# Two chained blocks on one core: GLA's output among RWKV's projections, and a new order of VectorE's work in the RWKV scan

## The chip, the cores and the metric

One core of a Trainium2 chip (trn2) runs the whole program in one launch. The metric is the device time of that launch in microseconds (us), the median of several runs. Times inside the program come from one profiled execution of the kernel before.

## What is computed

Two blocks run one after the other on 1024 tokens of 1024 channels in float32. Only the mixer of the first block matters here. It projects the normed tokens and gives half of the channels to a bidirectional gated linear attention (GLA, 4 heads) and half to a bidirectional RWKV-7 scan (8 heads), and concatenates the two:

```python
z = xn @ w_in[i]
z_rwkv, z_gla = z[..., :RWKV_IN_WIDTH], z[..., RWKV_IN_WIDTH:]
z_rwkv = z_rwkv + rwkv_mu[i] * (centred_shift(z_rwkv) - z_rwkv)
y_rwkv = rwkv7_mixer(z_rwkv, ...)      # two scans over time, S = S*w + (S@-kk) b^T + v k^T
y_gla = gla_mixer(z_gla, ...)          # ends with: o = rms_norm(o_f + o_b, norm_w) * silu(g)
y = jnp.concatenate([y_rwkv, y_gla], axis=-1) @ w_out[i]
```

The second block takes shifts and gains from a vector c through a 1024x6144 matrix ("ada" below); that product depends on nothing of the first block.

## The kernel before, in words

Each engine (PE = TensorE, DVE = VectorE, ACT = ScalarE, POOL = GpSimd, SP, which issues most transfers) runs its own instruction stream, written out by hand stage by stage. Every instruction counts up a semaphore of its engine, and `wait_ge` in front of an instruction holds the engine, with all that stands behind it, until named instructions or transfers are done. `meet` makes all engines wait for the ends of a stage. The stages around the change are `gla_scan`, `gla_out`, `rwkv_in` and `rwkv_scan`.

**GLA's output** (`gla_out_*`). The four heads' sums o lie in `g_o` (channels on partitions, 1024 tokens in the free dimension). ACT squares a head into one of two buffers `g_tmp`; PE sums it over the channels with two-column matmuls, 16 trace rows a head (`token_sums_pe`, L697). DVE and ACT form the inverse roots (`rsqrt_dve`, `rsqrt_act`). Then per head: DVE spreads the roots (`over_dve`, L685), PE turns them with eight 128x128 transposes into PSUM banks 6 and 7 (`over_pe`, L691), DVE multiplies o by norm and gate (L1159, L1161). All this is ahead of the stage's `meet`, and SP then stores `g_o` to DRAM as one transfer, `y_gla`.

**RWKV's projections** (`rwkv_in_*`). Fifteen blocks of the weight matrix, block j in two halves of 512 tokens, are multiplied on PE with operands split in a high and a low part: 24 matmuls for (j, 0) and 24 for (j, 1) (`split_pe`, L642 to L644). The weights come through a ring of three (SP, L594); ACT makes the high part of block j+2 behind PE's block j (`third_high_act`), DVE the low part (`third_low_dve`, L607), then reads block j out of PSUM, and shifts and mixes it with three more passes over 1024 tokens. Blocks 0 to 2 give `r_wlo`, `r_alo` and `r_sglo`. Between the halves PE does the jobs of the table `RJOBS`: ("sg", n) from (2, 1) on are decay products into banks 6 and 7, which DVE reads and ACT puts through a sigmoid; ("kk_sums", 0) at (7, 1) are 64 trace rows of two-column matmuls on the squared keys, the last square being made by ACT behind block 7.

ACT and POOL also work at ada in this stage, units q = 32 to 95: ACT scales a 128x512 piece of the matrix (L2532), POOL adds it to the sum (L2543), and ACT's next unit waits for that addition. ACT does the units of block j at the end of its work for j: `32 + 64*j//14` to `32 + 64*(j+1)//14`, so 4 or 5 a block from j = 0 on. Their buffers `aw` overlap `g_o`, so ACT first waits for the transfer `y_gla`. Behind (3, 1) PE sums the first finished group of eight, units 32 to 39 (`ada_sum_pe`, L2554, from the table `groups`), behind (5, 1) units 40 to 47, behind (6, 1) units 48 to 55.

**The RWKV scan** (`rwkv_scan_*`). 16 chunks of 64 tokens, 4 heads and both directions d at once. A turn u of the loop overlaps three chunks: the recurrence for u, the level products for m = u + 1, the Gram matrices for n = u + 2, and DVE's scaled operands for u + 3. The 64x64 triangular inverse of a chunk is made in steps. DVE masks the Gram matrices (`nm`, `mm`, L1717). The 16x16 diagonal blocks go by DRAM into `N16` on 32 partitions, and DVE inverts them in 15 levels of two short instructions (`substitute_dve`, L1673 and L1674), ahead of which it copies the identity (L1659). The result goes by DRAM into `ZZ` one turn later. Two more levels join 16 to 32 and 32 to 64: PE `p4`, DVE mask `t4` (L1737), PE `l4`, DVE `zz` (L1743), PE `p5`, DVE mask `t5` (L1750), PE `l5`, DVE `xt` (L1756). Transfers, in SP's order in a turn: `nm` out, then `ZZ` of the chunk before in (POOL issues half), `N16` in (POOL issues some), and later the inverted blocks out. DVE's order in a turn is: state update `S` (waits for PE's `ss`), masks, decay of S, y in the second half, products of u + 3 for d = 0, `t4`, products for d = 1, `zz`, identity and levels 0 and 1, `t5`, levels 2 to 4, `xt`, levels 5 to 14.

Of the kernel before, what the change touches and what calls it, by code (L numbers as in the profile page):

```python
# [211 lines left out]
class Kernel:  # L212
# [116 lines left out]
    def plan_block1(self):  # L329
# [225 lines left out]
    def pool_program(self):  # L555
# [583 lines left out]
    def gla_out_act(self):
        act = self.act  # L1140
        for h in range(4):
            if h >= 2:
# [2 lines left out]
        self.rsqrt_act("go", 64)
        for j in range(2):
            self.third_high_act("r", self.rw, self.rwkv_blocks(), j)
        self.meet(act, "gla_out")

    def gla_out_dve(self):  # L1150
        dve = self.dve
        self.rsqrt_dve("go", 64, [self.pe["go_sums", 3]], ALU.mult, 1.0 / PART, ALU.add, 1e-6)
        for h in range(4):
            y = self.g_o[:, h, :]
            if h >= 2:
                dve.wait_ge(self.pe["go%d" % (h - 2), "over"])
            self.over_dve("go%d" % h, self.st[:, 1, 16 * h:16 * h + 16].rearrange("p (b two) -> p b two", two=2)[:, :, 0:1], self.g_tmp[:, h % 2, :])
            dve.wait_ge(self.pe["go%d" % h, "over"])
            dve.c.scalar_tensor_tensor(out=two(y), in0=two(y), scalar=self.col("gla_norm"), in1=self.ps[:, 6:8, :], op0=ALU.mult, op1=ALU.mult) \  # L1159
                .then_inc(*dve.one("go", h))  # L1160
            dve.c.tensor_tensor(y, y, self.g_gate[:, h, :], ALU.mult).then_inc(*dve.one())  # L1161
# [144 lines left out]
    def rwkv_in_act(self):  # L1306
# [3 lines left out]
        act.wait_ge(self.t_keep["y_gla"])  # L1310
        for q in range(32, 36):
            self.ada_load_act(q)
        for j in range(15):
# [57 lines left out]
    def rwkv_in_dve(self):  # L1371
# [1882 lines left out]
```

## Time and profile before

| what | us |
|---|---|
| median of 3 runs | 3611.45 (3607.79 to 3614.22) |
| profiled execution, its own time | 3603.32 |
| its span, first to last instruction | 3602.0 |
| GLA's output, first sum to first projection | 419.29 to 458.71 |
| projections, up to the scan's first product | 458.71 to about 706 |
| RWKV scan | about 706 to 1106 |

The profile's times are microseconds from the first instruction. In a timeline row the first number is the start and the second the busy time of the row's instructions together ("x8" are eight); in brackets stands how long the engine stood idle before it and for whom. Matmul rows overlap, since they are pipelined. A float32 matmul shows as more than one row of the trace.

### The profile page before, as it was taken

Reading aid. Unit: us, or ns where it says so; the run is one execution under the profiler, and the core shown is the slowest. Engines: PE = TensorE matmul, PEld = TensorE weight load, DVE = VectorE, ACT = ScalarE, POOL = GpSimd, SP = SyncE. Lnnn points to the kernel's source line nnn. Section 1 sums busy time; section 2 is a strip of 40 time slices with the busy share of each in tenths; the row PEclk is TensorE's granted clock in tenths of the full one; section 3 lists DMA queues with packets and bytes.
Section 4 is the critical chain, followed back from the end, with each engine's and each line's share of the span. In section 5 each row is a group of like instructions: output and inputs, shape, how many; then the busy total and the mean of one; then the engine's idle time right before and its main releaser. Section 6 shows DMA issues by size and latency. Waiting matters only on the chain.

```text
span 3602.0 us, 56544 instructions
## 1 busy us (share of the span) xinstructions
PE 3262.9 (91%) x24603; PEld 2709.9 (75%) x24603; DVE 2270.9 (63%) x3114; ACT 1003.5 (28%) x1482; POOL 466.9 (13%) x362
## 2 busy tenths in 40 slices
PE   7988789888886999999999888998888899999996
PEld 5777767778885778888888667876676678888885
DVE  5758555678786444444444667996556566666666
ACT  4544233312113221111111452124454211211112
POOL 2520023322224000000000310000001001111110
PEclk9988698999998999999999999999999999999999
DMA  4410054322213111111110212122001111111111
GB/s 135 124 50 14 16 168 132 90 41 39 38 30 131 58 42 53 53 36 53 53 53 24 95 52 65 36 58 68 1 1 59 35 41 48 57 49 47 47 47 65
DMA packets 242719, 207.27 MB, mean 58 GB/s; under 512 B 66744, under 2 KB 205127, under 8 KB 241959
## 3 DMA queue, kind: packets, MB, share of 16 engines
q1 hardware_dynamic: 223527, 176.96, 16.4%
q10 hardware_dynamic: 13824, 25.17, 2.2%
q0 software_dynamic: 5120, 1.53, 0.4%
q8 instruction: 193, 3.16, 0.4%
q14 instruction: 55, 0.45, 0.0%
HBM read 172.06 MB, written 29.64 MB: 56 GB/s over the span
## 4 chain that ended last, share of the span: by engine, by line
PE 55%; DVE 8%; ACT 4%; issue 1%; POOL 0%; DMA 0%; DVEq 0%; SPq 0%; ACTq 0%; POOLq 0%
PE ps L2168 23%; PE ps L2183 16%; PE ps L2031 5%; PE ps L2916 2%; DVE Yc L2793 2%; PE ps L2892 2%; PE ps L642 1%; PE ps L643 1%; PE ps L644 1%; PE ps L2902 1%; PE ps L2893 1%; DVE e L2004 1%; ACT e L1986 0%; DVE small L1997 0%; POOL o_l L1780 0%
## 5 line engine op out<-in xcount | busy, mean ns | idle before, releaser
L3210 DVE TENSOR_TENSOR H<-H,ps 128x1024 f32<-128x1024 f32 x256 | 312.7, 1221 | 181.0 <-PE ps L2183 174.1
L2333 DVE TENSOR_TENSOR fsum<-fsum,ps 128x1024 f32<-128x1024 f32 x168 | 205.2, 1221 | 312.4 <-PE ps L2183 310.3
L2183 PE MATMUL ps<-dh,hh 128*128 128x512 f32 x864 | 339.9, 393 | 20.2 <-DVE hl L2148 14.2
L2183 PE MATMUL ps<-dl,hh 128*128 128x512 f32 x864 | 338.3, 392 | 0.0
L2183 PE MATMUL ps<-dh,hl 128*128 128x512 f32 x864 | 338.1, 391 | 0.0
L2168 PE MATMUL ps<-hn_h,uh 128*128 128x512 f32 x704 | 275.8, 392 | 7.2 <-DVE ul L1780 4.8
L2168 PE MATMUL ps<-hn_l,uh 128*128 128x512 f32 x704 | 275.3, 391 | 0.0
L2168 PE MATMUL ps<-hn_h,ul 128*128 128x512 f32 x704 | 275.3, 391 | 0.0
L2168 PE MATMUL ps<-hx_h,uh 128*128 128x512 f32 x512 | 200.5, 392 | 8.5 <-DVE hx_l L2148 5.3
L2183 PEld LDWEIGHTS ps<-dh,hh 128*128 128x128 f32 x864 | 163.7, 189 | 58.6 <-DVE hl L2148 15.9
L2168 PE MATMUL ps<-hx_l,uh 128*128 128x512 f32 x512 | 199.9, 390 | 0.0
L2168 PE MATMUL ps<-hx_h,ul 128*128 128x512 f32 x512 | 199.9, 390 | 0.0
L2183 PEld LDWEIGHTS ps<-dh,hl 128*128 128x128 f32 x864 | 163.5, 189 | 34.3
L2183 PEld LDWEIGHTS ps<-dl,hh 128*128 128x128 f32 x864 | 163.6, 189 | 33.6
L2543 POOL TENSOR_TENSOR a_x<-a_x,a_t 128x512 f32<-128x512 f32 x84 | 129.0, 1536 | 337.8 <-ACT a_t L2532 234.2
L3180 POOL TENSOR_TENSOR dw<-dw,g_row 128x1024 f32<-128x1024 f32 x32 | 78.7, 2461 | 707.4 <-DMA dw<-in_w_mlp_dram 707.4
L2168 PEld LDWEIGHTS ps<-hn_h,uh 128*128 128x128 f32 x704 | 133.1, 189 | 35.6 <-DVE ul L1780 5.2
L2793 DVE SCALAR_TENSOR_TENSOR Yc<-cp,cols,Yc 128x1024 f32<-128x1024 f32 x120 | 154.2, 1285 | 4.3
L2168 PEld LDWEIGHTS ps<-hn_l,uh 128*128 128x128 f32 x704 | 133.1, 189 | 27.7
L2168 PEld LDWEIGHTS ps<-hn_h,ul 128*128 128x128 f32 x704 | 133.0, 189 | 27.9
L642 PE MATMUL ps<-hx_h,cw 128*128 128x512 f32 x320 | 130.8, 409 | 17.2 <-DVE cw L622 7.5
L3189 ACT ACTIVATE relu<-ps 128x1024 f32<-128x1024 f32 x32 | 32.9, 1029 | 406.2 <-PE ps L2168 406.2
(474 smaller groups left out, 7626.8 us busy)
## 6 DMA issues: line engine op xcount, KB each, us to landing
aw<-in_w_ada_dram ACTq DMA_DIRECT2D x96, 256.0 KB, 3.0
uw<-in_w_mlp_dram SPq DMA_DIRECT2D x32, 512.0 KB, 4.2
dw<-in_w_mlp_dram SPq DMA_DIRECT2D x32, 512.0 KB, 5.1
uw<-in_ffn_gate_dram SPq DMA_DIRECT2D x22, 512.0 KB, 4.0
uw<-in_ffn_up_dram SPq DMA_DIRECT2D x22, 512.0 KB, 5.3
dw<-in_ffn_down_dram SPq DMA_DIRECT2D x22, 512.0 KB, 5.9
cw<-in_w_in_dram SPq DMA_DIRECT2D x20, 512.0 KB, 3.9
o_w<-in_w_out_dram SPq DMA_DIRECT2D x16, 512.0 KB, 9.9
```

The lines of the kernel that those rows point to most:

```text
L642: pe.e.matmul(ps[0:m, 2 * (j % 2) + h, :], wh[:, k, :], xh, start=(k == 0), stop=False)
L643: pe.e.matmul(ps[0:m, 2 * (j % 2) + h, :], wh[:, k, :], xl, start=False, stop=False)
L2031: mm = pe.e.matmul(self.ps[:, 2 * (t % 2) + hf, :], x[a](k), w[b](k)[:, half(hf)], start=(n == 0 and m == 0), stop=(n == len(order) - 1 an ...
L2168: mm = pe.e.matmul(ps[:, 2 * pair + h, :], w[:, col], x[h][v][:, k, :], start=(k == 0 and m == 0), stop=(k == DC - 1 and m == 2))
L2183: mm = pe.e.matmul(ps[:, 2 * pair + hf, :], v[s][:, blk(t)], w[:, half(hf)], start=(m == 0), stop=(m == 2))
L2333: return dve.c.tensor_tensor(f, f, new, ALU.add) if g else dve.c.tensor_copy(f, new)
L2543: pool.c.tensor_tensor(acc[:], acc[:], self.a_t[who][:], ALU.add).then_inc(*pool.one("ada", q, who))
L2793: dve.c.scalar_tensor_tensor(out=o, in0=x[:, w:w + TOK], scalar=self.col("dw", n + 4 * w), in1=o, op0=ALU.mult, op1=ALU.add) \
L2892: pe.e.matmul(ps[:, b, :], self.Qb[:, u, :], self.kr[:, u % 4, key:key + self.K8], start=True, stop=True)
L2916: mm = pe.e.matmul(ps[:, 6, blk(pr)], self.PT[u % 2][:, blk(j)], v, start=(j == 0), stop=(j == 5))
L3180: pool.e.tensor_tensor(w, w, self.g2_row[:], ALU.mult).then_inc(*pool.one("m", "dw", g))
L3210: return dve.c.tensor_tensor(h, h, self.ps[:, 4 + 2 * (t % 2):6 + 2 * (t % 2), :], ALU.add)
```

## The change

**GLA's output.** The stage's `meet` goes. Ahead of the projections PE keeps only the sums of heads 0 and 1. The sums of heads 2 and 3 stand behind (0, 0), and the four transposes of the inverse roots behind (0, 1), (1, 0), (1, 1) and (2, 0), in the order of heads 3, 0, 1, 2. DVE's products follow in `rwkv_in_dve`: one head ahead of block 0, two behind its mixing, the last behind the reading of block 1. ACT makes the high parts of blocks 0 and 1 between the squares. SP loads `r_wup` and `r_w0` behind the second head, and stores `y_gla` in its turn j = 1, behind the fourth. ACT waits for `y_gla` at the end of its work for j = 2, and then does units 32 to 40, nine of them, and five for each block after; `groups` stays. The first sg job waits for the fourth head. A third shift buffer `r_sh1` serves block 1.

**Scan.** On DVE both directions' products stand ahead of `t4`, and the identity copy too (`identity_dve`). The substitution starts behind `t5`: levels 0 to 3, then `xt`, then 4 to 14.

```diff
     def gla_out_pe(self):
-        for h in range(4):
-            pe.wait_ge(self.act["go_sq", h])
-            self.token_sums_pe(...)
-        for h in range(4):
-            if h:
-                pe.wait_ge(self.dve["go", h - 1])
-            self.over_pe("go%d" % h, NBLK, self.g_tmp[:, h % 2, :])
-        self.meet(pe, "gla_out")
+        for h in range(2):
+            self.gla_sums(h)
...
+    def gla_gated_dve(self, p):
+        dve, h = self.dve, self.GOUT[p]
+        y = self.g_o[:, h, :]
+        dve.wait_ge(self.pe["go%d" % p, "over"])
+        dve.c.scalar_tensor_tensor(... in1=self.ps[:, 6:8, :] ...).then_inc(*dve.one("go", p))
+        dve.c.tensor_tensor(y, y, self.g_gate[:, h, :], ALU.mult).then_inc(*dve.one("gated", p))
+        if p < 2:
+            self.gla_wide_dve(p + 2)
...  rwkv_in_sp
-        self.meet(sp, "gla_out")
-        sp.e.dma_start(self.dram["y_gla"], self.g_o[:]).then_inc(*self.t_keep.one("y_gla"))
+        sp.wait_ge(self.dve["gated", 1])
...
+            if j == 1:
+                sp.wait_ge(self.dve["gated", 3])
+                sp.e.dma_start(self.dram["y_gla"], self.g_o[:]).then_inc(*self.t_keep.one("y_gla"))
...  rwkv_in_pe
-            if (j, h) == (0, 1):
+            if (j, h) == (0, 0):
                 self.over_pe("xr", NBLK, self.r_sh[0][:])
+                for k in (2, 3):
+                    self.gla_sums(k)
+            elif j < 2 or (j, h) == (2, 0):
+                self.gla_over_pe(2 * j + h - 1)
...  rwkv_in_act
-        act.wait_ge(self.t_keep["y_gla"])
-        for q in range(32, 36):
-            self.ada_load_act(q)
+        self.rsqrt_act("go", 64)
...
-            for q in range(32 + 64 * j // 14, 32 + 64 * (j + 1) // 14 if j < 14 else 0):
+            if j == 2:
+                act.wait_ge(self.t_keep["y_gla"])
+                for q in range(32, 36):
+                    self.ada_load_act(q)
+            for q in range(32 + 64 * (j - 1) // 13 if j > 2 else 32, 32 + 64 * j // 13 if 2 <= j < 14 else 0):
                 self.ada_act(q)
...  rwkv_scan_dve
-            if u + 3 < NSUB:
-                products(u + 3, 0)
+            for d in range(2):
+                if u + 3 < NSUB:
+                    products(u + 3, d)
+            if n < NSUB:
+                self.identity_dve(n)
...
-            if n < NSUB:
-                self.substitute_dve(n, 0, 2)
...
-                self.substitute_dve(n, 2, 5)
+                self.substitute_dve(n, 0, 4)
...
-                self.substitute_dve(n, 5, 15)
+                self.substitute_dve(n, 4, 15)
```

Two places of the order of instructions. ACT from the end of GLA's output, before (`r_inv` is the copy behind the first transposes, `rwh` a block's high part, `aw` a load of an ada piece, `a_x` and `a_t` ada units):

```order
L1309 ACTIVATE r_inv_146<-ps 128x1024
L2520 DMA aw_59<-in_w_ada_dram 128x512
L2520 DMA aw_60<-in_w_ada_dram 128x512
L2520 DMA aw_61<-in_w_ada_dram 128x512
L2520 DMA aw_62<-in_w_ada_dram 128x512
L2145 ACTIVATE rwh_128<-rwr_127 128x1024
L2532 ACTIVATE a_x_63<-aw_59,cc_55 128x512
L2520 DMA aw_59<-in_w_ada_dram 128x512
```

And now, from the high part of block 2 on:

```order
L2172 ACTIVATE rwh_128<-rwr_127 128x1024
L2172 ACTIVATE rwh_129<-rwr_125 128x1024
L1333 ACT_TABLE_LOAD
L1333 ACTIVATE r_wlo_145<-r_wlo_145 128x1024
L2172 ACTIVATE rwh_128<-rwr_126 128x1024
L1301 ACT_TABLE_LOAD
L1301 ACTIVATE r_sg_149<-r_sg_149 128x1024
L2547 DMA aw_59<-in_w_ada_dram 128x512
L2547 DMA aw_60<-in_w_ada_dram 128x512
L2547 DMA aw_61<-in_w_ada_dram 128x512
L2547 DMA aw_62<-in_w_ada_dram 128x512
L2559 ACTIVATE a_x_63<-aw_59,cc_55 128x512
```

The loads of ada pieces, which stood ahead of everything for the blocks, now stand behind three high parts, the tanh of `r_wlo` and the first sigmoid of `r_sg`.

DVE in a turn of the scan, before, from `t4` on (`s_T` is `t4` or `t5`; `s_AR`, `s_BK`, `s_F`, `s_last` the products; `s_tmp` and `s_Z` the substitution):

```order
L1737 TENSOR_TENSOR s_T_172<-ps,lev_mask_161 128x256 [waits pe] x2
L1697 TENSOR_TENSOR s_F_178<-s_last_179,s_Ei_163 128x4 [waits dve]
L1698 TENSOR_TENSOR s_AR_182<-r_kk_143,s_Ex_165 128x4x64
L1699 TENSOR_TENSOR s_BK_196<-r_bb_142,s_En_164 128x4x64
L1700 TENSOR_TENSOR s_AR_182<-r_rkv_124,s_Ei_163 128x4x64
L1701 TENSOR_TENSOR s_BK_196<-r_rkv_124,s_En_164 128x4x64
L1702 COPY s_last_179<-s_Ei_163 128x4 [waits dve]
L1743 TENSOR_TENSOR s_ZZ_143_191<-s_ZZ_187,ps 128x512 [waits pe] x2
L1659 COPY s_Z_144_192<-eye_118_166 32x2x256 [waits dve,t_z]
L1673 TENSOR_TENSOR s_tmp_127_175<-s_N_119_167,s_Z_144_192 32x30 [waits dve,t_nb,t_n]
L1674 TENSOR_TENSOR s_Z_144_192<-s_Z_144_192,s_tmp_127_175 32x2x15 [waits dve]
L1673 TENSOR_TENSOR s_tmp_127_175<-s_N_119_167,s_Z_144_192 32x56 [waits dve]
```

And now, from the products of d = 1 on:

```order
L1726 TENSOR_TENSOR s_F_179<-s_last_180,s_Ei_164 128x4 [waits dve,pe]
L1727 TENSOR_TENSOR s_AR_183<-r_kk_144,s_Ex_166 128x4x64
L1728 TENSOR_TENSOR s_BK_197<-r_bb_143,s_En_165 128x4x64
L1729 TENSOR_TENSOR s_AR_183<-r_rkv_124,s_Ei_164 128x4x64
L1730 TENSOR_TENSOR s_BK_197<-r_rkv_124,s_En_165 128x4x64
L1731 COPY s_last_180<-s_Ei_164 128x4 [waits dve]
L1681 COPY s_Z_145_193<-eye_119_167 32x2x256 [waits dve,t_z]
L1769 TENSOR_TENSOR s_T_173<-ps,lev_mask_162 128x256 [waits pe] x2
L1773 TENSOR_TENSOR s_ZZ_144_192<-s_ZZ_188,ps 128x512 [waits pe] x2
L1777 TENSOR_TENSOR s_T_173<-ps,lev_mask_162 128x256 [waits pe] x2
L1702 TENSOR_TENSOR s_tmp_128_176<-s_N_120_168,s_Z_145_193 32x30 [waits t_nb,dve,t_n]
L1703 TENSOR_TENSOR s_Z_145_193<-s_Z_145_193,s_tmp_128_176 32x2x15 [waits dve]
```

The six products and the identity copy have moved from behind the first `s_T` to ahead of it, and the second `s_T` from behind two levels to ahead of all.

## Rows read from the trace of the kernel before

**Rows 1.** The page's first part: busy time, share of the span, instructions.
```profile
PE 3262.9 (91%) x24603; PEld 2709.9 (75%) x24603; DVE 2270.9 (63%) x3114; ACT 1003.5 (28%) x1482; POOL 466.9 (13%) x362
```

**Rows 2.** Windows: stretch, its us; PE, PEld, DVE, ACT, POOL busy; granted clock; DMA.
```profile
418.00:433.00 15.00, 13.71 (x64) 13.72 (x64) 0.00 (x0) 5.40 (x5) 0.00 (x0) 0.50 0.38 87
...
708.00:1075.00 367.00, 319.49 (x8176) 303.38 (x8175) 288.30 (x917) 69.61 (x148) 93.00 (x156) 0.96 0.21 38
```

**Rows 3.** Timeline of PE, GLA's output and the first projections.
```profile
419.29 13.78 PE L697 MATMUL ps<-ones,g_tmp 128*128 128x2 f32 x64 [2.16 <-ACT g_tmp L1144]
436.10 1.97 PE L691 MATMUL ps<-ident,g_tmp 128*128 128x128 f32 x8 [3.03 <-DVE g_tmp L685]
...
458.71 0.77 PE L642 MATMUL ps<-xs_h,rwh 128*128 128x512 f32 x1 [4.46 <-DVE rwl L607]
...
471.93 1.03 PE L691 MATMUL ps<-ident,r_sh 128*128 128x128 f32 x8
```

**Rows 4.** Timeline of DVE, the first head of GLA's output.
```profile
438.11 1.28 DVE L1159 SCALAR_TENSOR_TENSOR g_o<-g_o,cols,ps 128x1024 f32<-128x1024 f32 x1 [2.06 <-PE ps L691]
439.42 1.22 DVE L1161 TENSOR_TENSOR g_o<-g_o,g_gate 128x1024 f32<-128x1024 f32 x1
```

**Rows 5.** Timeline of ACT: loads, first ada unit, a table load, eighth unit.
```profile
473.11 1.79 ACTq L2520 DMA_DIRECT2D aw<-in_w_ada_dram  x4
...
476.75 0.73 ACT L2532 ACTIVATE a_x<-aw,cc 128x512 f32<-128x512 f32 x1 [0.74 <-DMA aw<-in_w_ada_dram]
...
485.65 1.28 ACT L1321 ACT_TABLE_LOAD   x1
...
495.24 0.72 ACT L2532 ACTIVATE a_t<-aw,cc 128x512 f32<-128x512 f32 x1 [1.50 <-POOL a_x L2543]
```

**Rows 6.** Timeline of PE in the projections: first ada sum, kk_sums.
```profile
509.02 0.95 PE L2554 MATMUL ps<-ones,a_x 128*128 128x2 f32 x8
...
577.57 7.63 PE L1245 MATMUL ps<-r_hsel,r_kk 128*128 128x2 f32 x35 [7.14 <-ACT r_kk L1328]
```

**Rows 7.** Timeline of DVE, one turn of the scan.
```profile
849.51 1.27 DVE L1717 TENSOR_TENSOR s_NM<-ps,gram_mask 128x512 f32<-128x512 f32 x2
...
857.02 0.89 DVE L1737 TENSOR_TENSOR s_T<-ps,lev_mask 128x256 f32<-128x256 f32 x2 [2.53 <-PE ps L1486]
...
859.56 1.28 DVE L1743 TENSOR_TENSOR s_ZZ<-s_ZZ,ps 128x512 f32<-128x512 f32 x2
...
862.32 0.74 DVE L1750 TENSOR_TENSOR s_T<-ps,lev_mask 128x256 f32<-128x256 f32 x2
...
864.66 0.73 DVE L1756 TENSOR_TENSOR s_XT<-s_ZZ,ps 128x256 f32<-128x256 f32 x2
...
873.05 0.42 DVE L1712 TENSOR_TENSOR s_S<-s_S,ps 128x256 f32<-128x256 f32 x1 [1.32 <-PE ps L1486]
```

**Rows 8.** DVE's `nm` masks over the scan: ns min/median/max, first and last start.
```profile
L1717 DVE TENSOR_TENSOR s_NM<-ps,gram_mask x32: 661/676/692, 709.8 to 1063.5; 128x512 f32<-128x512 f32 x32
```

**Rows 9.** Waits, 730 to 1060: who for whom, us in total, times, longest.
```profile
DVE s_T L1737 <- PE ps L1486: 34.9, 14, 3.8
...
DVE s_S L1712 <- PE ps L1486: 6.7, 9, 1.4
```

**Rows 10.** Transfers: destination, issuing queue, count, KB each, median us to landing.
```profile
rwr<-in_w_in_dram SPq DMA_DIRECT2D x14, 512.0 KB, 4.4
...
y_gla_dram<-g_o SPq DMA_DIRECT2D x1, 2048.0 KB, 8.1
```

**Rows 11.** Timeline of PE, start of `p4` in the next turn.
```profile
880.91 1.15 PE L1486 MATMUL ps<-s_ZZ,s_NM 64*64 64x64 f32 x32 [0.31 <-DMA s_ZZ<-zd_dram]
```

**Rows 12.** Timeline of DVE, the turn that has no products left.
```profile
1070.28 0.89 DVE L1737 TENSOR_TENSOR s_T<-ps,lev_mask 128x256 f32<-128x256 f32 x2 [3.63 <-PE ps L1486]
...
1072.93 0.69 DVE L1743 TENSOR_TENSOR s_ZZ<-s_ZZ,ps 128x512 f32<-128x512 f32 x1 [0.25 <-PE ps L1589]
...
1074.52 0.19 DVE L1673 TENSOR_TENSOR s_tmp<-s_N,s_Z 32x30 f32<-32x30 f32 x1 [0.38 <-DMA s_N<-nd_dram]
```

More of the change, by code:

```diff
@@ L1144, in gla_out_act, with gla_wide_dve @@
             act.e.activation(self.g_tmp[:, h % 2, :], self.g_o[:, h, :], ACTF.Square).then_inc(*act.one("go_sq", h))
[L1145 to L1148, printed above, removed]
-    def gla_out_dve(self):
[L1151 to L1161, printed above, removed]
+            if h % 2:
+                self.third_high_act("r", self.rw, self.rwkv_blocks(), h // 2)
+    def gla_wide_dve(self, p):
+        h = self.GOUT[p]
+        self.over_dve("go%d" % p, self.st[:, 1, 16 * h:16 * h + 16].rearrange("p (b two) -> p b two", two=2)[:, :, 0:1], self.g_tmp[:, p % 2, :])
+    def gla_gated_dve(self, p):
+        dve, h = self.dve, self.GOUT[p]
+        y = self.g_o[:, h, :]
+        dve.wait_ge(self.pe["go%d" % p, "over"])
+        dve.c.scalar_tensor_tensor(out=two(y), in0=two(y), scalar=self.col("gla_norm"), in1=self.ps[:, 6:8, :], op0=ALU.mult, op1=ALU.mult) \
+            .then_inc(*dve.one("go", p))
+        dve.c.tensor_tensor(y, y, self.g_gate[:, h, :], ALU.mult).then_inc(*dve.one("gated", p))
+        if p < 2:
+            self.gla_wide_dve(p + 2)
+    def gla_out_dve(self):
         for j in range(2):
             self.third_low_dve("r", self.rw, self.rwkv_blocks(), j)
-        self.meet(dve, "gla_out")
     RJOBS = {(2, 1): ("sg", 0), (3, 0): ("sg", 1), (3, 1): ("sg", 2), (4, 0): ("sg", 3), (4, 1): ("sg", 4), (5, 0): ("sg", 5), (5, 1): ("sg", 6), (6, 0): ("sg", 7),
@@ L1378, in rwkv_in_dve @@
         dve.e.tensor_scalar(self.r_omka[:], self.cols[:, ka:ka + 4], -1.0, 1.0, ALU.mult, ALU.add).then_inc(*dve.one())
-        dve.wait_ge(self.act["xr_inv"])
+        self.rsqrt_dve("go", 64, [self.pe["go_sums", 3]], ALU.mult, 1.0 / PART, ALU.add, 1e-6)
+        for p in range(2):
+            self.gla_wide_dve(p)
+        self.gla_gated_dve(0)
         for j in range(15):
             dst, mu, rows = self.rwkv_dst(j)
-            z, s = self.r_zp[j % 2], self.r_sh[j % 2]
+            z, s = self.r_zp[j % 2], self.r_sh[j % 2] if j != 1 else self.r_sh1
             dve.wait_ge(self.pe["r", j])
@@ L1397, in rwkv_in_dve @@
                 .then_inc(*dve.one("r_sh", j))
+            if j == 0:
+                self.gla_gated_dve(1)
+                self.gla_gated_dve(2)
             if j in (4, 6, 7, 9, 11, 12, 14):
@@ L1650, in rwkv_scan_pool, with identity_dve @@
         self.meet(self.pool, "rwkv_scan")
+    def identity_dve(self, n):
+        dve = self.dve
+        if n:
+            dve.wait_ge(self.t_z["out", n - 1])
+        dve.c.tensor_copy(self.Z16[:, :, 1], self.eye16[:]).then_inc(*dve.one("one", n))
     def substitute_dve(self, n, first, end):
@@ L1656, in substitute_dve @@
         if first == 0:
-            if n:
-                dve.wait_ge(self.t_z["out", n - 1])
-            dve.c.tensor_copy(self.Z16[:, :, 1], self.eye16[:]).then_inc(*dve.one())
+            dve.wait_ge(dve["one", n])
             dve.wait_ge(self.t_n["in", n], self.t_nb["in", n])
@@ L1737, in rwkv_scan_dve @@
                     dve.e.tensor_tensor(self.T[:, L[d]], self.hb(d, 0), rep(self.lev_mask[:, 0, d], 4), ALU.mult).then_inc(*dve.one("t4", m, d))
-            if u + 3 < NSUB:
-                products(u + 3, 1)
             if 0 <= m < NSUB:
```

19 lines of the change are left out of this document (14 added, 5 removed).

## The prediction

> **What bounds the kernel now.** I read the page's busy shares first: PE has work in 91% of the span [rows 1], so a change pays where PE idles or runs slowly. The windows show such stretches [rows 2]: during GLA's sums the granted clock is 0.50 (1.2 GHz); in the scan it is 0.96, and PE is busy 319 of 367 us. The timelines then say what the waits are for.
>
> *GLA's output.* PE starts the sums at 419.29 and the first projection at 458.71 [rows 3]. The 64 two-column rows take 13.8 us, 3.44 a head, and then the heads' transposes start 5.4 us apart: transposes 1.97, two products on DVE of 1.28 and 1.22, the rest spreading and hand-overs [rows 3, 4]. All of it lies on the path to the end.
>
> *Projections.* PE is dense, but ACT and POOL are nearly as full with ada. The first unit starts at 476.75, 3.6 us after the first load was issued, the eighth at 495.24 [rows 5]. PE's sum of these eight stands at 509.02 and waits for nothing; only ahead of kk_sums (577.57) does PE wait, 7.1 us for ACT, and the rows that follow have a pitch of 0.22 us, where the ada sum's have 0.11 [rows 6]: the half clock and the full one.
>
> *Scan.* A turn is a ring: `nm` is masked, SP fetches `ZZ`, PE makes `p4`, DVE masks `t4` and goes through ladder and substitution to S and the next `nm`. In the turn shown `nm` ends at 850.8, `t4` starts at 857.0 after 2.53 of idle time, and S could start at 871.7 but waits for PE to 873.05 [rows 7]. The masks go from 709.8 to 1063.5 over 15 turns, 23.6 us each [rows 8]. In 14 turns DVE waits 34.9 us ahead of `t4` and 6.7 ahead of S [rows 9].
>
> **GLA's output, step by step.** PE now does two heads ahead of the first projection: 2 x 3.44 from 419.3, so it starts at 426.2, if the weights are there. Their load is issued at 418.1 and lands in some 4.4 us [rows 10], high and low part take another 2.3: 424.8, in time. **Gain 32.5 us.** Then PE takes part of it back. Eight transposes at full clock show 1.03 us, 0.8 in pitch [rows 3]; four sets come into the projections, 3.2. The 32 sum rows cost 3.5 at the full clock's pitch [rows 6]. For a clock that falls there I add 2; the bounds are 0 and 5.8 (3.4 for the sums at the half clock, 2.4 for the start of a half block), and that GLA's 64 sums stay at 0.50 although they stand back to back [rows 2] says that such rows don't raise it.
>
> The Trainium skill (TensorE: Matmul & The Clock Gate, Part 4: PE-mode transpose) says that a transpose doesn't count as a busy PE. The eight at 471.93 run at full clock between dense matmuls, those at 436.10 take 1.97, which fits the rule without proving it. By the rule this term would be its upper bound, 5.8.
>
> **Who waits in between.** (0, 0) starts slowly as before and ends near 434, the sums near 440, (0, 1) near 446; a half block takes 5.5 (458.71 to 471.93 for block 0 [rows 3], less 2.4 for its slow start, halved). DVE's first head ends at 449.4, block 0 takes it 7.0 (low part, reading and three passes), the second head 2.5 [rows 4]: 458.9. Only then does SP issue the last small loads (3 us) and the fourth weight load. That lands at 466.4; high part, low part and reading of block 1 take 3.6, the fourth head 2.5: 472.6. PE loses 0.2 us at the first sg job and 2.2 at the second, and without ada would be behind (3, 1) at 486.8, where it was at 509.0: 22 us ahead.
>
> **There the lead is lost.** `y_gla` is issued at 472.7 and lands 8.1 us later [rows 10], at 480.8. ACT gets there at 481.2 and starts the first unit 3.6 us behind: 484.8. From the first to the eighth it was 18.5 us; I take off 2.3 for a table load (1.28) and a tanh that no longer stand between [rows 5]: 501.0, and POOL adds till 502.5. `groups` still asks for these eight behind (3, 1). So PE idles from 486.8 to 502.5 and keeps **6.5 us**. The nearest row for this is the old ada sum at 509.02; the units behind are chained one by one as before. Units 48 to 55 end with j = 5, and PE waits some 6 us more behind (6, 1), but that costs nothing: ACT's chain decides when kk_sums starts, 571 against 577.57. There the wait of 7.1 us goes, since PE has only just come through its block, and the 64 rows begin at the full clock. Half of them at 0.11 and not 0.22 is 3.5 us; the bounds are 0 and 7. Behind kk_sums nothing changes.
>
> **Output and projections together: 6.5 + 3.5 = 10 us less.** The low bound is 0, if `y_gla` or ACT is later by 7 to 10 us; the high one 23, if PE waited nowhere for ada (32.5 - 3.2 - 3.5 - 2, and 1 for the rest).
>
> **Scan, step by step.** No work is added. Ahead of `t4` go the products of d = 1 (1.6 us) and the identity copy (0.5), into an idle time of 2.5 on average [rows 9]: they are hidden by it, and would delay `t4` one for one if it were gone; I count 0.1. `t4` doesn't come earlier, as `p4` waits for `ZZ` [rows 11]. The turn without products shows the bare ladder: `zz` ends 3.34 behind the start of `t4` [rows 12], against 3.8 [rows 7]. `p5` of the second direction takes 0.6 and 0.15 of hand-over, `t5` 0.4: it ends at 4.5, before at 6.04. Then come four levels (2.0), `xt` (0.75), the fifth level (0.6) and what stood behind `xt` (865.4 to 871.7, 6.3): S can start 14.2 behind `t4`, before 14.7. PE starts `l5` 1.9 us earlier and is in time with `ss`, so that the 6.7 us ahead of S go. 14 x 0.5 + 6.7 = 13.7; the other way, a turn becomes 6.2 (to `t4`) + 14.2 + 1.95 (S and `nm`) = 22.35, 17.5 less over 14 turns. I take **14 us**. Bounds: 3, if the new waits for `l4` and `p5` are as long as the old one (2.5; of the ladder's 4.5 us DVE is busy 3.0), and 18. More is not to be had: the substitution needs `N16`, which came 10.4 us behind `nm` [rows 12], and now starts at 10.7.
>
> **The sum.** 10 + 14 = 24 us. From the profiled execution's 3603.3 that gives 3579.3. That execution is 8.1 us below the median of the runs; set against the median the forecast is 3611.4 - 24 = **3587 us**.
>
> **Rivals.**
>
> *A. The scan's new waits eat its gain.* For it: DVE now has nothing between `t4` and `zz`, and PE's slower moments all show. Against it: rows 12 have 0.25 of waiting for the second `zz`. 3611.4 - 10 - 3 = 3598.
>
> *B. The projections give nothing.* For it: ACT's ada chain starts 8 us later than before (484.8 for 476.75) and has to make it up; blocks with five units take 2.2 more than those with four. Against it: nine units now run in one piece. 3611.4 - 14 = 3597; with A as well 3608, no change.
>
> *C. The change doesn't meet a wait at (3, 1)*, because POOL adds faster than I read. All 23 us stay: 3611.4 - 37 = 3574. That the units wait for each other speaks against it.
>
> *D. Slower: PE's clock in the scan.* PE is busy 20.5 us a turn (319 of 367) at 0.96. At a granted clock g it takes 19.7/g, and some 3 of gaps come with the ladder. For it: the idle time gathers in fewer, longer pieces, and after one the clock has fallen before [rows 6]. It decides from the g at which the turn grows by the projections' 10 us over 14, to 24.3: 19.7/21.3 = 0.92. At 0.85 the turn is 26.2, 2.6 over today's, 36 us in all: 3611.4 - 10 + 36 = 3638. Against it: PE's idle time a turn shrinks by what the turn does.
>
> **How the numbers follow.** Forecast 0.48, A 0.15, B 0.14, A and B together 0.08, C 0.08, D 0.07. The predicted time is the forecast's. The range goes from 3570 (the high bounds of both parts, 41 us) to 3606 (2 or 3 us left of each), and leaves out D and half of A with B. Less than about 0.2%, 7.2 us, a measurement of this kernel can't tell from no change. Forecast, A, B and C lie beyond it, 0.85, of which 0.04 for their near ends falls within: faster 0.81, within 0.2% 0.12, slower 0.07.
>
> **What would show it.** Right: first projection near 426; the ada sum behind (3, 1) released by POOL near 502 after some 15 us; `y_gla` issued near 473; kk_sums near 571 without its wait, first rows at 0.11; in the scan `t5` ending 4.5 behind `t4`, no wait ahead of S, masks 22.4 to 22.6 apart. Wrong: no wait at (3, 1) (C), kk_sums still near 577 (B), 2.5 us a turn of waits for `zz` and `t5` (A), a clock in the scan below 0.92 (D).

## The result and the profile after

| | before | changed |
|---|---|---|
| median of the runs, us | 3607.79 (3605.29 to 3614.22, 5 runs) | 3590.73 (3584.53 to 3596.08, 5 runs) |
| ratio, 95% interval | | 0.9950, 0.9933 to 0.9967 |
| span of the profiled execution, us | 3602.0 | 3583.2 |
| mean granted clock | 0.948 | 0.949 |

The change saves 17 us, about 0.5%. (The median of before now includes two runs taken beside the changed kernel.) The forecast was 24 less, 3587 against the earlier median of 3611.45; the time measured lies in its range. Why 17 and not 24 is what follows.

The busy shares say little [rows 1]: the work is the same, and so are the shares.

```profile
PE 3261.7 (91%) x24603; PEld 2701.1 (75%) x24603; DVE 2268.1 (63%) x3114; ACT 1003.2 (28%) x1482; POOL 464.1 (13%) x362
```

TensorE's timeline of the changed kernel answers to rows 3 and 6. Line 697 are two-column sums, 642 the first matmul of a projection, 691 transposes, 1244 the sg jobs, 2581 the sums of ada's units, 1255 kk_sums (its row holds only the matmuls up to 580, the end of the window asked for).

```profile
415.58 6.96 PE L697 MATMUL ps<-ones,g_tmp 128*128 128x2 f32 x32 [2.16 <-ACT g_tmp L1152]
422.40 0.77 PE L642 MATMUL ps<-xs_h,rwh 128*128 128x512 f32 x1
...
429.52 1.03 PE L691 MATMUL ps<-ident,r_sh 128*128 128x128 f32 x8
430.39 3.63 PE L697 MATMUL ps<-ones,g_tmp 128*128 128x2 f32 x32
433.88 0.48 PE L642 MATMUL ps<-xs_h,rwh 128*128 128x512 f32 x1
...
474.84 1.13 PE L1244 MATMUL ps<-r_wup,r_wlo 64*128 64x512 f32 x4 [1.71 <-DVE r_sg L1358]
...
494.66 1.87 PE L2581 MATMUL ps<-ones,a_x 128*128 128x2 f32 x8 [13.03 <-POOL a_x L2570]
496.46 2.08 PE L1244 MATMUL ps<-r_wup,r_wlo 64*128 64x512 f32 x4
...
545.41 1.87 PE L2581 MATMUL ps<-ones,a_x 128*128 128x2 f32 x8 [5.56 <-POOL a_x L2570]
...
568.50 11.81 PE L1255 MATMUL ps<-r_hsel,r_kk 128*128 128x2 f32 x57 [2.19 <-ACT r_kk L1340]
```

The first sum stands 3.7 us earlier than before (415.58 for 419.29) although nothing ahead of it was changed, so I count from it. The first projection comes 6.8 behind it, before 39.4. The sum of ada's first eight units, now ahead of its data, waits 13 us for GpSimd, and the matmuls behind it (1.87 for 0.95, 2.08 for 1.13) run at the half clock. kk_sums starts 152.9 us behind the first sum, before 158.3: 5.4 of the 32.5 us are left. TensorE itself is ready for it 150.7 us behind the first sum, before 151.1; what has shrunk is its wait for ScalarE, from 7.1 us [rows 6] to 2.2. The rows of kk_sums still have a pitch of 0.21.

The windows of TensorE: stretch, its us, PE busy, granted clock, DMA share and GB/s.

```profile
427.00:434.00 7.00, 7.00 (x53) 1.00 0.01 2
...
560.00:590.00 30.00, 27.81 (x121) 0.72 0.22 63
701.00:1043.00 342.00, 305.54 (x7908) 0.98 0.22 38
```

Through the transposes and sums between the half blocks the clock stayed whole in this execution; around kk_sums it is 0.72, in the scan 0.98 for 0.96 [rows 2].

In the scan, the row of VectorE's `nm` masks answers to rows 8. They span 341.7 us against 353.7, 22.8 a turn for 23.6.

```profile
L1746 DVE TENSOR_TENSOR s_NM<-ps,gram_mask x32: 661/669/692, 701.3 to 1043.0; 128x512 f32<-128x512 f32 x32
```

VectorE's waits from 700 to 1045, for rows 9. Line 1769 is level four's mask `t4`, 1773 `zz`, 1777 level five's mask `t5`:

```profile
DVE s_ZZ L1773 <- PE ps L1613: 16.6, 28, 1.4
DVE s_T L1777 <- PE ps L1510: 6.2, 14, 0.5
DVE s_T L1769 <- PE ps L1510: 5.2, 9, 1.3
```

The 34.9 us ahead of `t4` have shrunk to 5.2 and the 6.7 ahead of S are gone, while 22.8 have appeared in the ladder. In all, 13.6 us of waiting less. One turn on VectorE's timeline, for rows 7:

```profile
842.71 0.89 DVE L1769 TENSOR_TENSOR s_T<-ps,lev_mask 128x256 f32<-128x256 f32 x2 [0.28 <-PE ps L1510]
844.43 0.69 DVE L1773 TENSOR_TENSOR s_ZZ<-s_ZZ,ps 128x512 f32<-128x512 f32 x1 [0.82 <-PE ps L1613]
845.36 0.69 DVE L1773 TENSOR_TENSOR s_ZZ<-s_ZZ,ps 128x512 f32<-128x512 f32 x1 [0.24 <-PE ps L1613]
...
846.83 0.42 DVE L1777 TENSOR_TENSOR s_T<-ps,lev_mask 128x256 f32<-128x256 f32 x1 [0.45 <-PE ps L1510]
847.39 0.19 DVE L1702 TENSOR_TENSOR s_tmp<-s_N,s_Z 32x30 f32<-32x30 f32 x1
...
856.89 0.73 DVE L1741 TENSOR_TENSOR s_S<-s_S,ps 128x256 f32<-128x256 f32 x2
857.56 1.26 DVE L1746 TENSOR_TENSOR s_NM<-ps,gram_mask 128x512 f32<-128x512 f32 x2
```

`t5` ends 4.5 us behind the start of `t4`, and S starts 14.2 behind it. Read so in all turns, S starts 14.14 to 14.19 us behind `t4` in 14 of 15 (15.5 in one), where before it was 14.4 to 16.0, 15.04 on average.

So the stretches give 3.7 us that are not the change's, 4.8 in the projections (285.7 us from the first sum to the first mask, before 290.5) and 12.0 in the scan, and 1.7 are lost behind it (2540.2 us for 2538.5, where the executions below scatter from 2537.1 to 2541.5 with the same code); 18.8 in all, the difference of the spans. The change's own part is some 17.

### The profile page after: what moved, and what is told of

Its sections match the earlier page's. It is cut to its first block, busy times and chain, and to the rows that moved or that the text cites. A ratio compares the mean times of both kernels' runs of the same rounds, so it can differ in the third digit from the quotient of the medians.

```text
span 3583.2 us, 56554 instructions
## 1 busy us (share of the span) xinstructions
PE 3261.7 (91%) x24603; PEld 2701.1 (75%) x24603; DVE 2268.1 (63%) x3114; ACT 1003.2 (28%) x1482; POOL 464.1 (13%) x362
## 4 chain that ended last, share of the span: by engine, by line
PE 56%; DVE 8%; ACT 4%; issue 1%; POOL 0%; DMA 0%; DVEq 0%; SPq 0%; ACTq 0%; POOLq 0%
PE ps L2195 23%; PE ps L2210 16%; PE ps L2058 5%; PE ps L2943 2%; DVE Yc L2820 2%; PE ps L2919 2%; PE ps L642 1%; PE ps L643 1%; PE ps L644 1%; PE ps L2929 1%; PE ps L2920 1%; DVE e L2031 1%; ACT e L2013 0%; DVE small L2024 0%; POOL o_l L1807 0%
## 5 line engine op out<-in xcount | busy, mean ns | idle before, releaser
L2210 PE MATMUL ps<-dh,hh 128*128 128x512 f32 x864 | 340.8, 394 | 17.9 <-DVE hl L2175 14.2
L2195 PE MATMUL ps<-hn_h,ul 128*128 128x512 f32 x704 | 275.3, 391 | 0.0
```

The source lines that it names most:

```text
L2195: mm = pe.e.matmul(ps[:, 2 * pair + h, :], w[:, col], x[h][v][:, k, :], start=(k == 0 and m == 0), stop=(k == DC - 1 and m == 2))
L2210: mm = pe.e.matmul(ps[:, 2 * pair + hf, :], v[s][:, blk(t)], w[:, half(hf)], start=(m == 0), stop=(m == 2))
```

## The experiments

Each experiment's profile is read by the same four stretches. Times in us; the ratio is to the kernel before, run beside it on the same chip.

| kernel | median | ratio (95%) | first sum at | from it to first mask | first to last mask | behind |
|---|---|---|---|---|---|---|
| before | 3607.8 | | 419.3 | 290.5 | 353.7 | 2538.5 |
| changed | 3590.7 | 0.9950 (0.9933 to 0.9967) | 415.6 | 285.7 | 341.7 | 2540.2 |
| e1 scan only | 3590.3 | 0.9958 (0.9941 to 0.9976) | 411.7 | 291.4 | 341.3 | 2541.5 |
| e2 output only | 3602.0 | 0.9995 (0.9980 to 1.0009) | 424.7 | 285.7 | 350.8 | 2538.8 |
| e3 sums later | 3586.5 | 0.9942 (0.9921 to 0.9963) | 421.2 | 285.0 | 347.7 | 2538.5 |
| e4 units spread | 3579.6 | 0.9930 (0.9909 to 0.9952) | 418.3 | 275.3 | 341.8 | 2540.5 |
| e5 load 3 first | 3578.9 | 0.9929 (0.9908 to 0.9949) | 418.5 | 280.4 | 341.5 | 2537.1 |
| e6 load 3, spread | 3572.6 | 0.9908 (0.9890 to 0.9927) | 424.1 | 268.8 | 341.2 | 2541.3 |
| e7 products only | 3589.0 | 0.9954 (0.9937 to 0.9972) | 419.7 | 285.7 | 340.0 | 2539.5 |
| e8 substitution only | 3604.3 | 0.9995 (0.9984 to 1.0006) | 425.0 | 285.7 | 355.8 | 2537.7 |
| e9 all three | 3569.8 | 0.9904 (0.9888 to 0.9920) | 420.7 | 266.7 | 339.9 | 2541.2 |
| e10 changed again | 3591.5 | 0.9958 (0.9941 to 0.9974) | 420.8 | 288.1 | 345.0 | 2540.2 |

The first column of stretches is noise: up to there all these kernels do the same, and it goes from 411.7 to 425.0.

**The two parts, each alone.** e1 is the kernel before with the scan's new order of VectorE, e2 the changed kernel with the old one.

> The kernel before, with only the scan's new order on VectorE. Theory (the two parts of the change are independent, and the scan gives most of it): the trace of the changed kernel shows 341.7 us from the first to the last mask of N where the kernel before has 353.7, so this kernel is 12 us faster than before (ratio 0.9967), masks 22.8 us apart, the first mask still near 709.8. Rival (the scan profits from what the projections leave behind, its clock or its transfers): masks stay over 23.2 us apart here and the gain is under 6 us.

> The changed kernel with the scan's old order, so only GLA's output is moved. Theory: 4.8 to 5.4 us less than before (ratio 0.9986), counted from GLA's first sum to the first mask of N; masks stay 23.6 us apart. In the changed kernel's trace the first sum itself stood 3.7 us earlier than before; if that belongs to one execution, it is somewhere between 415 and 419 here and the time tells nothing of it; if it belongs to the change, the sum is at 415.6 again and the gain is 8 to 9 us (0.9977). Rival: the projections give nothing, within 2 us of before.

e1 has the changed kernel's scan to half a microsecond (341.3) and, within the intervals, its whole gain. e2 has the changed kernel's first stretch exactly (285.7, 4.8 under before), but its time can't be told from before: the interval runs from 7 us less to 3 us more. So the scan gives most, the two are independent, and what the first part gives is seen in the trace alone. The 12 us of the scan are good to some 3: its old order spans 353.7 us in one execution and 350.8 in the other (e2, which I had expected at 23.6 a turn and which has 23.4), its new order 341.2 to 347.7 in the seven that have it unchanged. e2's first sum at 424.7 also settles that the earlier sum of the changed kernel belonged to one execution.

**What TensorE waits for at (3, 1).** First the sums alone are put later:

```
-        groups = dict(zip((3, 5, 6, 8, 10, 11, 13), range(4, 11)))
+        groups = dict(zip((4, 6, 7, 9, 10, 12, 13), range(4, 11)))
...
-            if j in (4, 6, 7, 9, 11, 12, 14):
+            if j in (5, 7, 8, 10, 11, 13, 14):
```

> The changed kernel with TensorE's sums of ada's units put one half block or more later: groups behind blocks 4, 6, 7, 9, 10, 12, 13 in place of 3, 5, 6, 8, 10, 11, 13. Theory 1 (the sum at (3, 1) is what TensorE waits for, nothing else is late there): the waits of 13.0 and 5.6 us for GpSimd are gone, and kk_sums starts 8 us earlier or more: 8 us less than the changed kernel, near 3583. Theory 2 (ScalarE's chain is the limit: the nine units of block 2 stand ahead of the high part of block 5, and VectorE's sg work comes behind): the wait of 13 us turns into waits at the next sg jobs and for the weights of block 5, and kk_sums moves by less than 4 us: 0 to 4 us less than the changed kernel.

The wait of 13 us went and came back 12.2 us long at the sg job right behind, now for VectorE. e3's TensorE, at the old place and at kk_sums (cut off at 580 again):

```profile
509.16 2.08 PE L1244 MATMUL ps<-r_wup,r_wlo 64*128 64x512 f32 x4 [12.23 <-DVE r_sg L1358]
...
572.62 7.63 PE L1255 MATMUL ps<-r_hsel,r_kk 128*128 128x2 f32 x35 [5.86 <-ACT r_kk L1340]
```

kk_sums moved from 152.9 to 151.4 us behind the first sum. That is the second theory: the data of that sum is only the first of several things that hang on ScalarE. ScalarE's timeline in the changed kernel shows the order: the high part of block 3, the loads of ada, nine units from 478 to 494, and only then the sigmoid of sg1 and the high part of block 5.

```profile
461.23 1.06 ACT L2172 ACTIVATE rwh<-rwr 128x1024 fp32r<-128x1024 f32 x1 [20.52 <-DMA rwr<-in_w_in_dram]
...
474.82 1.78 ACTq L2547 DMA_DIRECT2D aw<-in_w_ada_dram  x4
478.09 0.72 ACT L2559 ACTIVATE a_x<-aw,cc 128x512 f32<-128x512 f32 x1 [2.22 <-DMA aw<-in_w_ada_dram]
...
492.55 0.72 ACT L2559 ACTIVATE a_t<-aw,cc 128x512 f32<-128x512 f32 x1 [1.43 <-POOL a_x L2570]
...
494.81 1.06 ACT L1301 ACTIVATE r_sg<-r_sg 128x1024 f32<-128x1024 f32 x1 [0.41 <-ACT a_x L2559]
495.77 1.04 ACT L2172 ACTIVATE rwh<-rwr 128x1024 fp32r<-128x1024 f32 x1
```

e4 therefore deals the units out as well:

```
+    UNITS = (32, 32, 36, 41, 46, 52, 57, 62, 68, 73, 78, 84, 90, 96)
...
-            for q in range(32 + 64 * (j - 1) // 13 if j > 2 else 32, 32 + 64 * j // 13 if 2 <= j < 14 else 0):
+            for q in range(self.UNITS[j - 1], self.UNITS[j]) if 2 <= j < 14 else ():
```

> As the run before, with ScalarE's units of ada dealt out differently: 4 behind block 2 in place of 9, then 5 or 6 a block. Theory 2 (ScalarE's order is the limit at (3, 1)): the high part of block 5 comes 10 us earlier, the waits at (3, 1) and at the sg jobs behind it fall under 4 us together, and kk_sums starts 4 to 10 us earlier than in the changed kernel, as far as the six units a block further on don't make ScalarE late again; 4 to 10 us less than the changed kernel. Theory 3 (ScalarE is full from 478 to kk_sums, so the order doesn't matter): kk_sums stays within 2 us of the changed kernel, the wait stands elsewhere, and the time is the changed kernel's.

The waits shrank to 2.6 and 3.5 us (6.1 together, where I had expected under 4), kk_sums stands 143.0 behind the first sum, and the first mask comes 10.4 us earlier than in the changed kernel. e4's TensorE:

```profile
496.91 1.13 PE L1245 MATMUL ps<-r_wup,r_wlo 64*128 64x512 f32 x4 [2.64 <-DVE r_sg L1359]
507.19 1.87 PE L2582 MATMUL ps<-ones,a_x 128*128 128x2 f32 x8 [3.49 <-POOL a_x L2571]
...
561.32 13.82 PE L1256 MATMUL ps<-r_hsel,r_kk 128*128 128x2 f32 x64 [3.40 <-ACT r_kk L1341]
```

It is the same 64 units on the same ScalarE, so their place was the loss. But the place that counts need not be the one behind block 2 that theory 2 names. e4's list also leaves fewer units ahead of kk_sums. ScalarE's units from 460 to 575, ahead of kk_sums in each kernel, are these and four writes of `a_x` more, in the kernel before, the changed one and e4:

```profile
L2532 ACT ACTIVATE a_t<-aw,cc x28: 704/724/727, 477.9 to 572.0; 128x512 f32<-128x512 f32 x28
```

```profile
L2559 ACT ACTIVATE a_t<-aw,cc x25: 709/722/728, 479.2 to 561.1; 128x512 f32<-128x512 f32 x25
```

```profile
L2560 ACT ACTIVATE a_t<-aw,cc x21: 705/723/727, 485.0 to 554.6; 128x512 f32<-128x512 f32 x21
```

That is 32 units before, 29 in the changed kernel and in e3, and 25 in e4. e4 differs from e3 in that list alone, and its kk_sums comes 8.4 us earlier; four units at the 2.15 us from one to the next (488.24, 490.39, 492.55 in the changed kernel) are 8.6, an estimate. So the four units that moved behind kk_sums can account for nearly all that e4 gains over e3, and the sums moved later for the other 1.5. Behind kk_sums the displaced units cost nothing: from its start to the first mask it is 132.3 us, in the changed kernel 132.8. Neither theory had counted them. What a better order of the same 29 units would give by itself isn't shown; no run has that.

**The fourth weight load.** In the changed kernel SyncE issues it behind its wait for GLA's second head, and ScalarE waits 20.5 us for it (the row at 461.23 above). e5 issues it ahead of that wait, e6 does so with e4's edits.

```
+        self.third_load_sp("r", self.rw, blocks, 3)
         sp.wait_ge(self.dve["gated", 1])
...
-            if j + 3 < 15:
+            if 3 < j + 3 < 15:
```

> The changed kernel with SyncE's load of weight block 3 issued ahead of its wait for GLA's second head, so beside the small loads. In the changed kernel ScalarE waited 20.5 us for it and VectorE 6.3 behind ScalarE. Theory (this load is the first late thing, and all of ScalarE's ada chain stands behind it): VectorE's 6.3 us go, y_gla is issued and ScalarE's first unit comes 4 to 6 us earlier against GLA's first sum, the waits of 1.3 and 1.7 us at the first two sg jobs go, and the first mask of N stands 4 to 5 us nearer to GLA's first sum than the 285.7 us of the changed kernel; the time is 4 us less. Rival (ScalarE's units are limited by GpSimd further on): first mask of N within 1 us of 285.7.

> Weight block 3 ahead of the wait, and the sums and units of the run with 4 units behind block 2, which had its first mask of N at 275.3 us behind GLA's first sum and waits of 2.6, 3.5, 2.8 and 3.4 us left on TensorE up to kk_sums. Theory (the same ScalarE chain is still the limit, by what these waits show): 3 to 5 us more, first mask 270 to 272 behind the first sum, near 3576. Rival: the waits left are for GpSimd's chain of units, which starts earlier too but has no slack: 1 us or nothing.

The waits went as expected, the sizes only in part. In e5 the waits at the first two sg jobs are gone, VectorE's 6.3 us are 0.3, and the wait at (3, 1) is 11.3; but ada's first unit comes 60.4 us behind the first sum for 62.5, 2.1 earlier and not 4 to 6. This execution lost 3.2 us to the clock behind the second sums (the last section), the changed kernel's none. kk_sums starts 2.4 us earlier, its rows took 2.2 us less, and the first mask stands 5.3 earlier, so that the 5.3 are the edit and the clock together. By the ratios its time is 8 us under the changed kernel's, but the two intervals overlap. In e6 the first mask stands 268.8 behind the first sum, 6.5 under e4 where I had expected 3 to 5; 1.6 of that are the clock, which e4 lost behind its second sums and e6 did not. Its first unit comes 56.9 behind the first sum, 5.6 earlier than in the changed kernel, with neither of them losing there. The load's gain adds to e4's.

**The two halves of the scan's edit.** e7 keeps the products and the identity copy ahead of level four and puts the substitution back:

```
+            if n < NSUB:
+                self.substitute_dve(n, 0, 2)
...
-                self.substitute_dve(n, 0, 4)
+                self.substitute_dve(n, 2, 5)
...
-                self.substitute_dve(n, 4, 15)
+                self.substitute_dve(n, 5, 15)
```

e8 does the opposite:

```
-            for d in range(2):
-                if u + 3 < NSUB:
-                    products(u + 3, d)
-            if n < NSUB:
-                self.identity_dve(n)
+            if u + 3 < NSUB:
+                products(u + 3, 0)
...
+            if u + 3 < NSUB:
+                products(u + 3, 1)
+            if n < NSUB:
+                self.identity_dve(n)
```

> The changed kernel with only one half of the scan's edit: both directions' products and the identity copy ahead of level four, the substitution in its old places (levels 0 and 1 ahead of level five's mask, 2 to 4 behind it). Theory (the gain is that the ladder from t4 to t5 carries no product any more; in the changed kernel VectorE waits 16.6 us for zz and 6.2 for t5, and two levels, 0.8 us a turn, cost nothing there): first to last mask of N 337 to 343 us, as much as the whole edit (341.7) or a little more. Rival (the gain is that level five's mask comes ahead of the substitution): 349 us or more, where the old order has 350.8 to 353.7.

> The other half: direction 1's product and the identity copy stay between t4 and zz, the substitution starts behind level five's mask. Theory: zz of the first direction comes 2 us behind where it could, t4's wait comes back at some 1.6 us a turn more than the 5.2 us in all of the changed kernel, and the wait for zz (16.6 us) is filled: 345 to 349 us from the first to the last mask of N, a gain of some 5 us against the old order. Rival (this half is the whole gain): 342 us.

e7 has the whole gain of the scan and 1.7 us more (e9, with the same scan, 1.8), which is less than the new order scatters by, so that the single turns below are the better evidence; e8 has none, its masks span 355.8 us, which is more than I expected of it. The masks of e7 and then of e8:

```profile
L1746 DVE TENSOR_TENSOR s_NM<-ps,gram_mask x32: 667/672/692, 705.4 to 1045.4; 128x512 f32<-128x512 f32 x32
```

```profile
L1746 DVE TENSOR_TENSOR s_NM<-ps,gram_mask x32: 667/671/692, 710.7 to 1066.5; 128x512 f32<-128x512 f32 x32
```

The reason stands in the waits. In e8 the 36.4 us ahead of `t4` are back (line 1766) and the ladder has next to none (line 1778 is `t5`), so that the product again lengthens the way from `t4` to S: 15.2 us a turn, where the changed kernel has 14.2 and e7 13.6.

```profile
DVE s_T L1766 <- PE ps L1510: 36.4, 14, 3.6
...
DVE s_T L1778 <- PE ps L1510: 4.5, 25, 0.2
```

A turn of e7, where two levels of the substitution lie in the wait for `t5`, and one of the four slow ones:

```profile
844.50 0.89 DVE L1769 TENSOR_TENSOR s_T<-ps,lev_mask 128x256 f32<-128x256 f32 x2
846.22 0.69 DVE L1773 TENSOR_TENSOR s_ZZ<-s_ZZ,ps 128x512 f32<-128x512 f32 x1 [0.82 <-PE ps L1613]
...
849.35 0.19 DVE L1702 TENSOR_TENSOR s_tmp<-s_N,s_Z 32x30 f32<-32x30 f32 x1 [1.51 <-DMA s_N<-nd_dram]
...
860.30 0.42 DVE L1741 TENSOR_TENSOR s_S<-s_S,ps 128x256 f32<-128x256 f32 x1 [0.40 <-PE ps L1510]
```

S comes 13.6 us behind `t4` in 10 of 15 turns, 0.6 earlier than in the changed kernel, and now waits for TensorE again, 2.4 us in all. In four turns it takes 14.7 to 15.1, so that only 1.7 us of the 15 times 0.6 show. In three of the four VectorE waits 1.2 to 1.6 us at the first level for the transfer of `N16`, as in the row at 849.35; in the fourth the granted clock was 0.88. The changed kernel, whose substitution starts later, has such a wait only once, of 3.9 us in its first turn. So the old place of the substitution wins 0.6 us a turn as long as `N16` has landed, and its landing is the next limit.

**All of it, beside the changed kernel.**

> Weight block 3 ahead of the wait, 4 units behind block 2 with the later sums, and in the scan only the products ahead of level four with the substitution in its old places. Theory (the three edits lie in different stretches, so their gains add): first mask of N 268.8 us behind GLA's first sum, 340 us to the last mask, so 1 us under the run without the last edit and some 18 us under the changed kernel; ratio to before 0.990. Rival (the scan's old substitution places cost when it starts at another clock): 343 us or more between the masks.

> The changed kernel itself, once more and beside the run above on one chip. Theory (what differs from one execution to the next lies ahead of GLA's first sum): 285.7 us from that sum to the first mask of N and 341.7 to the last, whatever the whole time is; ratio to before 0.995. Rival (the kernel's scatter sits in the changed stretches too): either of the two is off by more than 2 us.

e9 combines e6 and e7. At 3569.8 it is some 35 us under before (ratio 0.9904) and 22 under the changed kernel beside it, and so beats both; its ratio and e6's can't be told apart, and only the trace has the last 3 us (266.7 and 339.9), of which 2.1 lie in a stretch where the two kernels are the same. e10 contradicts its theory: 288.1 and 345.0 in place of 285.7 and 341.7. The changed stretches have some scatter of their own. The section on the hardware traces 1.6 of the 2.4 us and about half of the 3.3 to the clock.

## Why the prediction came out right, where by luck, and where its 7 us went

- **Bound, and the 32.5 us: right.** The first projection starts 6.8 us behind the first sum, forecast 6.9.
- **The four transposes and the sums: right.** Eight transposes take 1.03 us and the 32 sum rows 3.63, as counted. **The 2 us for a clock that falls there** were 0 in this execution, 1.6 to 3.2 in four others (below).
- **The lead lost at (3, 1): right in kind, 4 us off in size.** The step said that GpSimd's last sum lets TensorE go at 502.5 after 15.7 us. Counted from the first sum that is 83.2; measured 79.1, after 13.0. Two terms were too long: the first unit came 62.5 behind the first sum (forecast 65.5), since `y_gla` was issued 1.5 us earlier than forecast and ScalarE issued ada's loads 7.4 us behind it, not 8.5; and from first to eighth unit it was 14.5 us, not 16.2. What the step missed is e3's finding: the block's high part and the sigmoid stand behind the same nine units, so that moving the sum alone wins 1.5 us.
- **What carries the lead to kk_sums: wrong, and the number right by luck.** The forecast took 6.5 us, the lead left at the sum at (3, 1), as kk_sums' lead, since "the units behind are chained one by one as before". At (3, 1) the lead was 10.7 us and not 6.5, and at kk_sums 5.4. The old sum at 509.02 waited for nothing, so a lead over it says nothing of ScalarE's chain; the eighth unit comes 77.0 us behind the first sum now, 76.0 before. And the units are not as before: three fewer stand ahead of kk_sums, 29 for 32, which the forecast passed over. ScalarE's first unit comes 5.0 us later, the stretch from it to the last one ahead of kk_sums takes 83.0 us for 95.3, and the last square follows that unit 1.9 later, by a wait for TensorE: 5.4 us less in all. Three units at 2.15 us are 6.5 us of the 12.3, an estimate, and more than the whole gain; the rest about balances the later start. So it isn't shown that moving GLA's output, with 32.5 us of lead at its start, earns anything at kk_sums by itself; the kernel before with nothing but three units put behind kk_sums was not run.
- **kk_sums' rate: wrong.** The step that failed is "the 64 rows begin at the full clock", with half of them at a pitch of 0.11. TensorE still waits 2.2 us for ScalarE ahead of them, and 5.6 at (6, 1), as forecast. The rows take 13.3 us for 13.8: 0.5 gained of the 3.5 forecast. I had written that the wait of 7.1 us goes and concluded the full clock from that; a wait of 2.2 was left, and in the changed kernel it was followed by the half clock. That such a wait always costs it isn't shown: in e5 the same 2.2 us were followed by 64 rows in 11.1 us, in e9 2.7 us by 13.8. "Behind kk_sums nothing changes" was 1.1 us off too: the granted clock was 0.63 over the 14 us from 680, ahead of the scan, where it was 0.76 over the 14 from 690 before. Together the projections gave 4.8 us (5.4 + 0.5 - 1.1), not 10.
- **Scan: mechanism right, 12 us and not 14.** `t5` at 4.5, S at 14.2, no wait ahead of S: all as worked out. Over the 14 turns between the masks that have an S, the way from the start of `t4` to the next `nm` shrank by 14.8 us, forecast 13.7. The mis-sized term is the way from `nm` to `t4`. I took it as unchanged and from the one turn shown, where it is 7.5 us from start to start; over these turns it averaged 7.8 before and 7.9 in the changed kernel, 2.1 us more in all, and the first turn, which has no S, took 0.7 more (20.7 for 20.0). That makes 12.0. I had counted 0.1 a turn for the products ahead of `t4` and left it out of the sum; whether they are the cause isn't shown, since e8, with the product of d = 1 back behind `t4`, has 7.9 too, and e6, with it ahead, 7.8. A turn became 22.9 us and not 22.35, low by the 0.4 between 7.5 and 7.9 and by 0.1 for the one slow turn. The forecast did not see that of the two halves only the first earns anything (e7, e8): it added the substitution's new place without asking what lies in the ladder's waits instead.
- **Rivals.** A (waits in the ladder eat the gain) has its waits, 22.8 us of them, 1.6 a turn, but not its price: 12 us are left and not 3. e7 shows that two levels belong into them. B is refuted by the trace, though e2's time alone could not refute it. C is refuted by the wait of 13.0, D by a granted clock of 0.98.

The Trainium skill (TensorE: Matmul & The Clock Gate, Part 4: PE-mode transpose) says that a transpose doesn't count as a busy PE in the same way as other matmuls. By that rule the clock term would have been its upper bound, an estimate of 5.8 us from this case's rows. The runs lie between the rule and no effect: nothing in six executions, 1.6 to 3.2 us in four.

## What to carry to other kernels

When an engine's early start pulls a join forward, look at the chain of the engine that feeds it, not only at the join itself: moving the join won 1.5 us, putting four more of the units behind the next landmark that waits for that engine, where it had time to spare, 8.4. Count the units ahead of such a landmark before and after an edit, or a gain is put down to the wrong cause. Give an order its fillers where the waits are: work that no one waits for goes ahead of a chain, and a piece of the next chain into the waits within it, as far as its data has landed. And take a ring's length from all its turns, not from one.

## What the runs showed of the hardware

**Scatter from the clock, ahead of the change.** The first sum stands anywhere from 411.7 to 425.0 us with the same work in front of it. The granted clock of 50 us windows in GLA's scan differs from one execution to the next, here e1 (first sum at 411.7) and then before (419.3) from 250 to 300:

```profile
250.00:300.00 50.00, 40.58 (x904) 1.00 0.07 19
```

```profile
250.00:300.00 50.00, 42.24 (x743) 0.83 0.04 13
```

Over the twelve profiled executions it goes the same way in the main: from 200 to 410 the granted clock is 0.89 in e1, the earliest, and 0.83 to 0.84 in the three latest (e2, e6 and e8, first sum at 424.1 to 425.0), though it is 0.83 in the kernel before too, with its sum at 419.3. A single execution thus shifts by up to 13 us for nothing, three quarters of what the change is worth. The stretch from one landmark to the next repeats far better.

**Transposes and sums between dense matmuls.** From the start of the second 32 sums to the next transposes it is 9.05 us in the changed kernel, e2, e6, e7, e8 and e9, and 10.6 to 12.3 in e3, e4, e5 and e10. In e10 the matmuls behind the sums take 0.63 us and not 0.39 till 443.4, and the windows show the clock:

```profile
436.00:440.00 4.00, 4.00 (x39) 1.00 0.02 4
440.00:444.00 4.00, 4.00 (x13) 0.57 0.00 0
444.00:448.00 4.00, 4.00 (x23) 1.00 0.00 0
```

TensorE was never idle there: the same sequence of instructions costs 0 or 1.6 us or, in e5, 3.2, from one execution to the next. The forecast's 2 us was a fair price for a term that one trace can't settle.

**Slow turns in the scan.** S starts 14.2 us behind `t4` in most turns of the new order and 15.4 to 15.7 in a few: one of 15 in the changed kernel, two in e10, five in e3, whose masks span 341.7, 345.0 and 347.7 us. All eight had a granted clock of 0.89 from `t4` to S. The slow turn of e10 at 828 beside an ordinary one at 783, where the clock was 1.00:

```profile
783.00:799.00 16.00, 15.04 (x414) 1.00 0.21 49
...
828.00:844.00 16.00, 15.57 (x389) 0.89 0.13 38
```

The three slow turns of e7 that wait for `N16` are of another kind: in two of them the clock was 1.00. What lets the clock fall in one execution and not in the other stays open; no run here was made for it.
